# One more projection chunk by seven half-sized products in a one-core decoder layer

## What is computed

```python
proj = h @ w_in                       # h = RMSNorm(x): 264 x 1024, w_in: 1024 x 6400
xin, bg, cg, q, k, v, g_conv, g_attn = split(proj)
conv_out = causal_depthwise_conv3(cg * xin)
y_conv = bg * conv_out
y_attn = sliding_window_attention(rms(q), rms(k), v, bias, sinks)
merged = sigmoid(g_conv) * y_conv + sigmoid(g_attn) * y_attn
x = x + merged @ w_out
x = x + moe(RMSNorm(x))               # top 4 of 32 experts, 403 MB of expert weights
```

## Time and profile before

| | |
|---|---|
| median of 3 runs | 1148.14 us (1147.71 to 1148.73) |
| the profiled execution's own time | 1147.19 us |
| its span, first to last instruction | 1145.4 us |
| granted TensorE clock, mean | 0.993 |
| PE busy | 1097.6 us (96%) |
| DVE busy | 437.5 us (38%) |
| ACT busy, POOL busy | 188.0 us, 88.4 us |
| bytes moved by DMA | 444.36 MB |

### The profile page before, as it was taken

One profiled execution on the slowest core, in us unless ns is written; L12 is line 12 of the kernel. 1 busy time (PEld: TensorE's weight loads), 2 busy tenths in 40 slices (PEclk: granted clock), 3 DMA queues, 4 the chain that ended last, 5 costly groups with the idle time before them and its releaser, 6 DMA issues.

```text
span 1145.4 us, 15065 instructions
## 1 busy us (share of the span) xinstructions
PE 1097.6 (96%) x6055; PEld 497.1 (43%) x6055; DVE 437.5 (38%) x858; ACT 188.0 (16%) x398; POOL 88.4 (8%) x161
## 2 busy tenths in 40 slices
PE   9999999999999999999898999999999999999997
PEld 6689898543333333333333333333333333333332
DVE  4577786753433223233223232323232323232322
ACT  2133341221321101010101010101010101010101
POOL 1785215000000000000000000000000000000000
PEclk9999999999999999999999999999999999999999
DMA  9947629999999999999999999999999999999997
GB/s 313 314 128 186 210 85 353 416 357 425 400 420 426 419 432 431 430 433 431 433 433 429 434 430 433 435 428 434 429 434 431 431 434 429 435 429 434 425 423 287
DMA packets 53206, 444.36 MB, mean 388 GB/s; under 512 B 13101, under 2 KB 19373, under 8 KB 35741
## 3 DMA queue, kind: packets, MB, share of 16 engines
q1 hardware_dynamic: 46712, 435.83, 91.7%
q0 software_dynamic: 5600, 7.32, 2.4%
q10 hardware_dynamic: 852, 0.64, 0.2%
HBM read 439.78 MB, written 2.37 MB: 386 GB/s over the span
## 4 chain that ended last, share of the span: by engine, by line
PE 62%; DMA 37%; DVE 0%; issue 0%; ACT 0%; ACTq 0%; SPq 0%; DVEq 0%
PE pA L2051 32%; PE pB L2051 21%; DMA ring<-in_w_up 21%; DMA ring<-in_w_down 10%; PE pM L2051 6%; DMA area<-in_w_up 5%; PE pM L2054 1%; PE pA L2054 1%; DMA x<-in_x_prompt 1%; ACT area L1269 0%; DVE x L1898 0%; SPq L800 0%; DVE conv_row L1812 0%; DVE area L1973 0%; DVE x L1978 0%
## 5 line engine op out<-in xcount | busy, mean ns | idle before, releaser
L2051 PE MATMUL pA<-ring,hn 128*64 128x512 f32 x1536 | 352.6, 602 | 23.0 <-DMA ring<-in_w_up 23.0
L2051 PEld LDWEIGHTS pA<-ring,hn 128*64 128x64 f32 x1536 | 105.3, 137 | 218.8 <-issue 185.5
L2051 PE MATMUL pB<-ring,area 128*64 128x512 f32 (+2 forms) x784 | 171.5, 591 | 6.6 <-DMA ring<-in_w_down 5.8
L2051 PE MATMUL pA<-area,hn 128*64 128x512 f32 x512 | 119.3, 610 | 10.4 <-DMA area<-in_w_up 10.4
L2051 PE MATMUL pB<-area,ring 128*128 128x132 f32 (+2 forms) x928 | 126.4, 327 | 0.0
L2051 PEld LDWEIGHTS pB<-area,ring 128*128 128x128 f32 (+1 forms) x928 | 106.7, 175 | 18.2 <-issue 2.3
L2051 PEld LDWEIGHTS pB<-ring,area 128*64 128x64 f32 (+2 forms) x784 | 58.5, 136 | 101.2 <-issue 87.8
L1898 DVE TENSOR_TENSOR x<-pM,x 128x512 f32<-128x512 f32 x60 | 40.1, 691 | 147.7 <-PE pM L2051 147.7
L1257 ACT ACTIVATE area<-area 128x512 f32<-128x512 f32 x30 | 18.9, 631 | 385.2 <-DVE area L1881 385.2
L1812 DVE COPY conv_row<-pM 128x512 f32<-128x512 f32 x30 | 20.6, 686 | 146.0 <-PE pM L2051 146.0
L2051 PEld LDWEIGHTS pA<-area,hn 128*64 128x64 f32 x512 | 36.2, 139 | 74.5 <-issue 59.7
(11 more groups left out here) (348 smaller groups left out, 907.1 us busy)
## 6 DMA issues: line engine op xcount, KB each, us to landing
ring<-in_w_up SPq DMA_DIRECT2D x36, 4096.0 KB, 29.8
ring<-in_w_down SPq DMA_DIRECT2D x18, 4096.0 KB, 29.0
area<-in_w_up SPq DMA_DIRECT2D x12, 4096.0 KB, 30.2
ring<-in_w_up SPq DMA_DIRECT2D x16, 2048.0 KB, 13.4
area<-in_w_down SPq DMA_DIRECT2D x6, 4096.0 KB, 30.0
ring<-in_w_in SPq DMA_DIRECT2D x22, 1024.0 KB, 10.0
ring<-in_w_down SPq DMA_DIRECT2D x16, 1024.0 KB, 11.6
ring<-in_w_up SPq DMA_DIRECT2D x16, 1024.0 KB, 8.4
```

The costliest lines, as they stand in the source:

```text
L2051: return pe.matmul(out, w, m, start=start, stop=stop, skip_group_check=True)
```

## The change

Chunk 8, the second half of xin, joins `SEVEN`. Its four tiles become seven slots and it gets four weight sums. Since it comes behind cg (chunk 7), which lies in `cx`, its quarters are multiplied in place there, and a new semaphore `quarters_made` tells ACT when a channel group is complete for `first_tap`. Its sums take one more place of the ring, so the loads of chunks 9, 10 and 11 wait for one `ring_free` more each (7, 8, 9 where it was 6, 7, 8); those of 8, 12, 13 and 14 wait as before. The tables are written anew for the steps around it.

```diff
-SEVEN = (3, 5, 6, 7, 9, 10, 11, 12)
+SEVEN = (3, 5, 6, 7, 8, 9, 10, 11, 12)
...
-              (slot(7, 0), slot(7, 0), slot(7, 1), slot(7, 2), 30, slot(9, 3), slot(9, 5)),
-              (slot(9, 3), slot(9, 4), slot(9, 5), slot(10, 0), slot(10, 2), slot(11, 1), slot(11, 3))]
-SECOND_TURNS = (slot(7, 0), slot(9, 3))
+              (slot(7, 0), slot(7, 0), slot(7, 2), slot(7, 3), slot(8, 0), slot(9, 4), slot(9, 6)),
+              (slot(9, 3), slot(9, 5), slot(9, 6), slot(10, 0), slot(10, 2), slot(11, 1), slot(11, 3))]
+SECOND_TURNS = (slot(7, 1), slot(9, 4))
...
-FIRST_TAP_STEPS = [15, 16, 17, 17, 30, 31, 32, 33]
-TAP_STEPS = [16, 17, slot(5, 0), slot(5, 0), 31, 32, 33, slot(9, 0)]
+FIRST_TAP_STEPS = [15, 16, 17, 17, slot(8, 5), slot(8, 5), slot(8, 6), slot(8, 6)]
+TAP_STEPS = [16, 17, slot(5, 0), slot(5, 0), slot(8, 6), slot(8, 6), slot(9, 1), slot(9, 1)]
...
-             9: (slot(7, 5), slot(7, 6), slot(7, 6), 30),
-             10: (31, slot(9, 0), slot(9, 1), slot(9, 2)),
+             8: (slot(7, 4), slot(7, 5), slot(7, 6), slot(8, 0)),
+             9: (slot(8, 1), slot(8, 2), slot(8, 3), slot(8, 4)),
+             10: (slot(9, 1), slot(9, 2), slot(9, 6), slot(10, 0)),
...
                     if a == 0:
                         act.wait_ge(v_moved, 16 * 16)
...
-                    n = TILES.index(("xin", 4 if a < 4 else 8, a % 4, a))
-                    act.wait_ge(tile_free_dve, DVE_TILES[n] + 1)
+                    c = 4 if a < 4 else 8
+                    if c in SEVEN:
+                        act.wait_ge(quarters_made, MADE_BEFORE[c] + (2 if a % 4 < 2 else 3))
+                        act.wait_ge(tile_free_dve, DVE_READ[c, "c12"])
+                    else:
+                        act.wait_ge(tile_free_dve, DVE_TILES[TILES.index(("xin", c, a % 4, a))] + 1)
...
                     dve.wait_ge(tile_free_dve, DVE_READ[c, name])
-                    out = quarter(yc, c, name)
-                    link(V.tensor_tensor(out, g, out, ALU.mult))
+                    if xin:
+                        out = quarter(cx[:, :, 2:], c, name)
+                        V.tensor_tensor(out, g, out, ALU.mult).then_inc(quarters_made, 1)
+                        dve.wait_ge(quarters_made, MADE_BEFORE[c] + ("c22", "c12", "c21").index(name) + 1)
+                    else:
+                        out = quarter(yc, c, name)
+                        link(V.tensor_tensor(out, g, out, ALU.mult))
```

More of the change, by code:

```diff
@@ L243, in plan @@
         after[SPLIT_STEPS[n]].append(("split", n))
+    assert not any(after[n] for n in range(len(TILES)) if TILES[n][1] in SEVEN)
     steps = [("anorm", 0), ("s_cols", 0)]
@@ L331, in counts @@
             for name in ("r1", "c11", "w", "c22", "c12", "c21"):
-                if name != "c11" or kind == "bg":
+                if name != "c11" or kind in ("bg", "xin"):
                     d += 1
@@ L347 @@
 counts()
+MADE_BEFORE = {4: 0, 8: 3 * (4 in SEVEN)}
 AFTER_XIN = [c for c in SEVEN if STEPS.index(("slot", (c, 0))) > STEPS.index(("sides", 4))]
@@ L600, in build @@
         tap_ready = sem("tap_ready")
+        quarters_made = sem("quarters_made")
         state_tapped = sem("state_tapped")
@@ L1394, in place_of @@
                     return quarter(cx[:, :, 2:], c, name) if plain else g
+                xin = TILES[2 + 4 * (c - 1)][0] == "xin"
                 def times(name, g):
@@ L1412, in seven @@
                         dve.wait_ge(sig_used, GATED[c - 1, "c21"])
+                    elif c - 1 in SEVEN:
+                        dve.wait_ge(tile_free_dve, DVE_READ[c - 1, "c21"])
                     read("r1", r1, t1, bank_y)
                 elif s == 2 and not (gated or plain):
-                    out = quarter(yc, c, "c11")
+                    if xin:
+                        dve.wait_ge(tile_free_act, ACT_DONE[c - 1, "c11"])
+                        dve.wait_ge(tile_free_dve, DVE_READ[c - 1, "c21"])
+                    out = quarter(cx[:, :, 2:] if xin else yc, c, "c11")
                     V.tensor_tensor(out, pairs_of(bank_x), out, ALU.mult).then_inc(tile_free_dve, 1)
```

## The result

The changed kernel takes 1149.91 us (median of 21 runs, 1148.36 to 1152.52), the kernel before, run beside it, 1148.14 us (21 runs). The ratio is 1.0014, with a 95% interval of 1.0008 to 1.0020: 1.8 us slower (0.9 to 2.3), and not faster. The forecast was 1149.2. The profiled execution took 1150.54 us, with a span of 1148.7 us.

A forecast was written before the change was run, and what follows sets the result against it. PE was taken to be the limit in the touched stretch, setting the expert weight stream's start. A gain of 1.64 us and a wait of 2.7 us gave +1.06, 1149.2 us against the median; range 1146.5 to 1151.4.

The forecast's parts named there:

- The gain: Chunk 8 on PE: seven slots take 12.60 us where the tiles took 14.24, a gain of 1.64 us.
- DVE up to chunk 9's slot 4: DVE busy 19.05 of 22.89 us up to there; the edits cost nothing, last read about 1.3 us ahead.
- The list from c22 to r1: DVE work from chunk 9's slot 4 to chunk 10's r1: 13.42 us, so PE waits 2.7 us at slot 3.
- The moved probabilities: Unit 2's moves behind chunk 11's load: there at 150.0 us, first turn wants them at 151.49, no wait.
- the middle estimate: Chunk 11's load lands in 6.2 us, unit 2's last move 3.9 us behind it, at 151.0, still in time.
- Rival 1: Moves land late at chunk 9's first turn, delay added to r1's wait in full: 1149.7 to 1152.7 us; chance 0.18.
- Nothing is added there: Behind chunk 10's r1, PE and DVE go on as before, with nothing added and nothing won back.
- The sum: -1.64 + 2.7 = +1.06 us on the profiled execution's 1147.19; against the median 1148.14 it is 1149.2 us.
- the forecast's own case: Wait of 2.3 to 3.1 us at chunk 10's slot 3, moves in time: 1148.8 to 1149.6 us; chance 0.58.
- no wait comes at `r1`: Chunk 10's slot 3: gain kept, 1146.5 us; kept wholly or in part 1146.5 to 1148.3, chance 0.16.
- the stream of weights hides what PE loses: The weight stream sets the end by itself, gain and wait both hidden: 1148.1 us; chance 0.08.

The follow-up runs named there:

- The kernel without waits: Changed kernel with unit 2's moves ahead of chunk 11's load, two weight sums behind r1, unit 2's turns behind chunk 9's slot 3: 1146.16 us, ratio 0.9983.
- the order alone: Kernel before, chunk 8 left in four plain tiles, only turns, bias, peak, values and two weight sums moved as in the change: 1151.70 us, ratio 1.0031.
- moves ahead: Changed kernel with unit 2's moves ahead of chunk 11's load in SP's queue instead of behind it: 1149.20 us, ratio 1.0010.
- the filler: Changed kernel with six unused matmuls ahead of PE's wait for r1: 1149.99 us; again, beside the change's 1150.21 us, 1148.92 us.
- the longer wait: Changed kernel with chunk 10's fourth weight sum computed three times in place of once, without extra matmuls: 1153.93 us.

## Why the prediction was right

**The gain.** 1.64 us were forecast for chunk 8, and the slots took the 12.60 us that the sum used. The kernel without waits gained 1.51 us in the profiled stretch.

**DVE up to chunk 9's slot 4.** Said to cost nothing, with 1.3 us to spare. DVE waited 1.09 us for slot 4, and PE for nothing in chunks 8 and 9 up to there.

**The list from c22 to r1.** 13.42 us were added up. From 149.86 to 163.87 are 14.01 us, of which 0.99 us is the wait for the moves, so the list itself took 13.02 us; the kernel with the order alone has 13.06. The overlap of unlinked instructions was taken as up to 0.3 us and was 0.4. The wait at slot 3 was to be 2.7 with the moves in time; it was 2.50 where they were (moves ahead, the order alone) and 2.59 in the change, and moving two sums out of the list took away 2.27 of it. This step was right, and it is what turned the gain into a loss: with the order alone the same wait comes without chunk 8's seven products, and with the sums moved chunk 8's gain is visible.

**The moved probabilities.** Here the sum failed. Its term was no wait, with the last move there at 150.0 us against 151.49. Shifted by the 0.7 us by which this profile runs ahead (126.94 against 127.63 in the chains), that is 149.3 against 150.8; it was there at 151.6, 0.99 us after the turn wanted it, and 2.3 us after the sum. Two prices were off. I took landing in 2.1 us from moves that had the queue to themselves; behind a load the last took 3.6 us, near unit 1's 3.9, which stood in the middle estimate. And the ten issues took 7.8 us, not 6.5. A third slip hid part of it: the sum counted the landing from the end of the last issue, 0.6 us too late; counted from its start, as here, 148.0 and 3.6 give 151.6, and the turn began at 151.74. The middle estimate had its 3.9 about right; its load was to land in 6.2 us, and the second half took 7.7. Rival 1 thus came in part. It was to add to the wait at slot 3 in full; it showed as 0.79 us ahead of the values, since PE comes by there first, and both together are 3.38 us, 0.88 more than with the moves in time.

**The clock.** No step of the prediction had it. "Nothing is added there" was wrong: behind the wait of 2.59 us, slots 3 to 6 took 8.97 us in the profile in place of 7.2. The Trainium skill (TensorE: Matmul & The Clock Gate, section Part 1) describes two levels and a throttle that comes back when the engine has been idle. The trace agrees, at 0.50 and 1.00, and the filler shows that it is the idle time that brings it. Slots 3 to 6 took 8.90 to 8.97 us in the three profiles of the change and 7.30 in the two of the filler, so there the clock costs 1.6 to 1.7 us. How often it comes in ordinary executions with this wait stays open: not in all, by the two at a mean of 1.000, and the medians put its average cost at 1.29 us beside the filler in one set and at nothing between two sets.

**The sum.** The forecast was -1.64 + 2.7 = +1.06. With the measured waits it is -1.64 + 0.79 + 2.59 = +1.74, and with the clock as in the profile about +3.5, near the +3.75 of the profiled stretch; the medians say +1.77 and +2.03, each known to about 1 us or a little less. So the direction and the mechanism were right, and the size was short by a wait of up to 0.8 us and by a cost of the clock that the medians do not fix. That 1149.91 came within 0.7 us of 1149.2 with two losses left out is in part luck. It lies above the forecast's own case (1148.8 to 1149.6), in the part of rival 1's band that was thought least likely, and the whole range was wide enough to hold no change as well.

**The other rivals.** That no wait comes at `r1` fell with the 2.59 us. That the stream of weights hides what PE loses fell twice: the loads went out 3.05 us later in the profile, and 2.5 us more of wait, with its clock, cost more than 2.5 us in the median. What frees the stream's first loads, PE's pace at chunks 11 and 12, passed the shifts on: in the twelve profiles the first expert load moved by -2.0 to +5.2 us against the profile before, and the end of the span moved with it to within 1.2 us.

## What to carry to other kernels

Where one engine sets the end and another feeds it, add up the second one's instructions between two points that the first one sets, in the order in which they stand: here 13 us of DVE work had to fit into 11 us of PE work, and the share of busy time (38%) said nothing of it. Work that is moved off one wait lands in front of another; ask of each moved piece what the next read behind it is, and put what is needed late (here two weight sums) behind that read. Small transfers behind a load of 2 MB in one queue landed here with the load or after it, so give them their place in the queue by when they are ready. And where TensorE is the limit, ask what its clock does behind a wait: in the profiles here a wait of 2.5 us cost 1.6 to 1.8 us more than itself.

## What the runs showed of the hardware

At chunk 10's slot 3 the granted clock fell to 0.50 in all six profiles that have a wait of 2.50 us or more there (the change three times, moves ahead, the order alone, the longer wait), and behind none of the waits of 0.82 us or less in the stretch. It fell between half a microsecond before PE began to work again and 1.1 us after that, and slots 3 to 6 of chunk 10 took 8.7 to 9.0 us in place of 7.2. Unused matmuls in the wait kept it at 1.00. I had not expected this of a wait so short.

Waits in between lie in the experts' part, where PE waits for weights, and there the clock fell behind some of them only. PE's timeline of the kernel before:

```profile
678.18 3.65 PE L2051 MATMUL pA<-area,hn 128*64 128x512 f32 x16 [1.85 <-DMA area<-in_w_up]
707.32 3.65 PE L2051 MATMUL pA<-ring,hn 128*64 128x512 f32 x16 [1.29 <-DMA ring<-in_w_up]
736.47 5.35 PE L2051 MATMUL pA<-ring,hn 128*64 128x512 f32 x16 [1.85 <-DMA ring<-in_w_up]
765.61 3.65 PE L2051 MATMUL pA<-ring,hn 128*64 128x512 f32 x16 [0.95 <-DMA ring<-in_w_up]
```

Four of its nine waits of 1.85 to 1.87 us have the 5.35 us behind them, at a clock of 0.50, and none of the nine in the changed kernel's profile. That is why the mean granted clock is 0.993 in the profile before and 0.998 in the one of the change, although only the change has the fall at slot 3. In the experts' part it moved nothing that the rows show: the next load's matmuls begin 29.1 us later either way, behind a wait of 0.95 in place of 1.29 us. The same lower clock is paid for at slot 3, since PE is the limit there.

Moves of 32 KB behind a load of 2 MB were also slow to be issued: ten took SP 7.8 us in the changed kernel, 6.5 us in the kernel before, and 7.1 us (133.09 to 140.27) where they stood ahead of the load. What made the rest of the difference was not looked into.
